# State part of an RWKV-7 mixer on 64x64 diagonal blocks, the convolution's chunks before the value's, ten of its taps on VectorE

## Chip, cores and metric

One core of a Trainium2 chip runs the whole program in one launch. The metric is device microseconds of that core, median of several executions. The engines named are TensorE (PE; PEld is its weight load), VectorE (DVE), ScalarE (ACT), GpSimd (POOL) and SyncE (SP, which issues the DMAs).

## What is computed

Two transformer layers on 256 tokens of width 1024, in float32. The first (attention, pooling mixer, gated feed-forward) is not touched. The second has a mixer of a causal depthwise convolution (512 channels, 31 taps) with layer norm and SiLU, and an RWKV-7 state of 8 heads of 64 channels, then a PEER feed-forward over 16384 experts. What the change touches is this part of the mixer:

```python
y = a * sigmoid(b)                     # 512 channels each, from w_in
y = depthwise_conv(y, w_dw) + b_dw     # 31 taps, causal
y_conv = silu(layernorm(y) * ln_w + ln_b)

def step(state, inp):                  # for each of 256 tokens, 8 heads, state 64x64
    r_t, k_t, v_t, w_t, kk_t, a_t = inp
    sa = einsum('bhij,bhj->bhi', state, -kk_t)
    state = state * w_t[:, :, None, :] + sa[..., None] * (kk_t * a_t)[:, :, None, :] \
            + v_t[..., None] * k_t[:, :, None, :]
    return state, einsum('bhij,bhj->bhi', state, r_t)
y = groupnorm(scan(step)) + bonus      # then * g, and concat(y_conv, y_rwkv) @ w_out
```

## The kernel before

Every large product goes over weight chunks of 128x1024 float32. SyncE loads them into a ring of four buffers (`raw`), ScalarE rounds each to `w_hi` (L497), VectorE subtracts to `w_lo` (L911, `split`), and TensorE makes three products of each 128x128 piece (L1511 to L1513). A chunk of the second layer's input projection (`MIX`, 22 chunks, `mix`) gives 128 channels x 256 tokens in one PSUM bank; ScalarE takes it out (`mix_taken`, L686) and VectorE adds the shifted token (`shift`, L1117). The order is lora inputs, k, r, v (chunks 10 to 13), the convolution's gates (14 to 17), its inputs (18 to 21). `conv_in` (L1188) is input times gate, in `cy`.

The state is computed in chunks of 64 tokens. A unit of work is a block b = 2t + h%2 (t: 128 tokens, that is two chunks; four heads k). First the factors Z, B, K and V are transposed to token-major (L1800) and taken out by ScalarE (`tok_major`, L736). The Gram products (L1814) of 128 tokens against 128 are masked by VectorE (L1208) to within 64x64 diagonal blocks, so that half of each 128x128 tile is zero. `NEUMANN` is a list of ten steps of one or two products that invert the triangular matrix; for each step, all four blocks: products (L1836, L1834 where a mask follows, L1832 a transpose) into banks 2b and 2b+1, evicted by ScalarE ("act", 36 of them, L759) or VectorE ("add", "copy", "eye" or a mask, 36, L1228, L1223, L1225, L1230). A block waits for its own evictions of the step before (`DONE`). Then m1 (L1843), m1T (L1848), w1 (L1854), m2 (L1860), phi (L1869) and u (L1877, L1878), the three rounds over chunk states (`phi_state`, L1891; L1903 `sa`), y (L1916, L1918, L1919), and y's group norm (L1923, L1761, L1769). Then the eight chunks of `w_out` (`W_OUT2`).

Beside the state part runs the convolution: ScalarE multiplies two tiles of 256 tokens by a tap's weight (`tap_pair`, L744, two instructions) into a ring of three pairs, GpSimd adds the pair to `co` (L1498). Sixty pairs are the 30 taps beyond the first; eight come in front of the Neumann loop, one or two behind each of ScalarE's evictions. The layer norm of `co` (sums on TensorE, L1885 and L1895) is issued among the chunk states. All engines work through their own queue in the order written; semaphores order them between each other. `w_out` chunks 3 to 7 are loaded after the Neumann loop, as D2U and D2L lie in `raw`.

## Time and profile before

| what | us |
|---|---|
| median of 3 runs | 1558.61 (1556.29 to 1560.1) |
| the profiled execution, its own time | 1559.9 |
| its span in the trace | 1558.1 |
| last chunk of the input projection ends | 544.0 |
| Gram products start | 548.7 |
| Neumann products | 554.8 to 626.6 |
| first chunk of `w_out` starts | 679.5 |

A row of a timeline has the start in us from the span's start, the length of the group, engine, line and operation, output and inputs, shapes, and how many records were merged; in brackets the idle time before it and what ended it. Each float32 matmul of TensorE leaves two records. Lengths of TensorE's records are modelled and overlap, so the distance between starts is what a record costs the engine. `PEclk` in a window is the granted clock as a share of 2.4 GHz.

### The profile page before, as it was taken

Reading aid. Unit: us, or ns where it says so; the run is one execution under the profiler, and the core shown is the slowest. Engines: PE = TensorE matmul, PEld = TensorE weight load, DVE = VectorE, ACT = ScalarE, POOL = GpSimd, SP = SyncE. Lnnn points to the kernel's source line nnn. Section 1 sums busy time; section 2 is a strip of 40 time slices with the busy share of each in tenths; the row PEclk is TensorE's granted clock in tenths of the full one; section 3 lists DMA queues with packets and bytes.
Section 4 is the critical chain, followed back from the end, with each engine's and each line's share of the span. In section 5 each row is a group of like instructions: output and inputs, shape, how many; then the busy total and the mean of one; then the engine's idle time right before and its main releaser. Section 6 shows DMA issues by size and latency. Waiting matters only on the chain.

```text
span 1558.1 us, 29537 instructions
## 1 busy us (share of the span) xinstructions
PE 1494.1 (96%) x10922; PEld 1367.6 (88%) x10922; DVE 1007.9 (65%) x1777; ACT 847.7 (54%) x1587; POOL 214.1 (14%) x128
## 2 busy tenths in 40 slices
PE   5999989999989999998999999999999999999997
PEld 5967979999969998888999999999999888888885
DVE  5454557665666764446996588888997555555554
ACT  5444546555546598334544456777775544544543
POOL 0030000000000089004788300000000000000000
PEclk9999999999999999999999999999999999999999
DMA  6545565666744400125556654444446666666661
GB/s 240 171 149 203 165 228 181 205 214 213 257 149 134 124 1 1 56 72 186 156 184 186 184 185 150 136 141 144 136 143 195 190 195 194 190 194 196 190 193 62
DMA packets 68365, 252.89 MB, mean 162 GB/s; under 512 B 7584, under 2 KB 7840, under 8 KB 67488
## 3 DMA queue, kind: packets, MB, share of 16 engines
q1 hardware_dynamic: 67104, 245.40, 49.6%
q10 hardware_dynamic: 1152, 5.98, 1.0%
q8 instruction: 76, 1.25, 0.3%
q14 instruction: 33, 0.27, 0.0%
HBM read 249.25 MB, written 2.10 MB: 161 GB/s over the span
## 4 chain that ended last, share of the span: by engine, by line
PE 89%; DVE 5%; ACT 3%; issue 3%; POOL 0%; DMA 0%; ACTq 0%; DVEq 0%; POOLq 0%
PE bank L2002 22%; PE bank L1511 18%; PE bank L1512 17%; PE bank L1513 17%; PE bank L1968 4%; PE bank L1544 2%; PE bank L1836 1%; DVE arena L932 1%; PE bank L1834 1%; DVE w_lo L911 1%; ACT arena L744 0%; PE bank L1953 0%; DVE arena L929 0%; POOL arena L1498 0%; PE bank L1559 0%
## 5 line engine op out<-in xcount | busy, mean ns | idle before, releaser
L1511 PE MATMUL bank<-x_hi,w_hi 128*128 128x256 f32 x2120 | 620.4, 293 | 19.2 <-DVE x_lo L942 6.3
L911 DVE TENSOR_TENSOR w_lo<-raw,w_hi 128x1024 fp32r<-128x1024 f32 x364 | 445.6, 1225 | 262.4 <-ACT w_hi L497 259.3
L1512 PE MATMUL bank<-x_lo,w_hi 128*128 128x256 f32 x2120 | 603.5, 285 | 0.0
L1513 PE MATMUL bank<-x_hi,w_lo 128*128 128x256 f32 x2120 | 603.2, 285 | 0.0
L497 ACT ACTIVATE w_hi<-raw 128x1024 fp32r<-128x1024 f32 x416 | 439.1, 1056 | 184.3 <-PE bank L2002 167.2
L1511 PEld LDWEIGHTS bank<-x_hi,w_hi 128*128 128x128 f32 x2120 | 409.8, 193 | 51.3 <-issue 36.3
L1512 PEld LDWEIGHTS bank<-x_lo,w_hi 128*128 128x128 f32 x2120 | 410.8, 194 | 0.4
L1513 PEld LDWEIGHTS bank<-x_hi,w_lo 128*128 128x128 f32 x2120 | 410.1, 193 | 0.0
L2002 PE MATMUL bank<-w_hi,x_hi 128*128 128x512 f32 x508 | 156.4, 389 | 0.0
L2002 PE MATMUL bank<-w_lo,x_hi 128*128 128x512 f32 x508 | 156.4, 389 | 0.0
L2002 PE MATMUL bank<-w_hi,x_lo 128*128 128x512 f32 x508 | 156.3, 389 | 0.0
L1473 POOL TENSOR_TENSOR w_lo<-raw,w_hi 128x1024 fp32r<-128x1024 f32 x52 | 125.3, 2411 | 120.6 <-ACT w_hi L497 120.6
L1498 POOL TENSOR_TENSOR arena<-arena 128x512 f32<-128x512 f32 x60 | 75.7, 1306 | 452.8 <-ACT arena L744 452.8
L2002 PEld LDWEIGHTS bank<-w_lo,x_hi 128*128 128x128 f32 x508 | 95.3, 188 | 19.9
L2002 PEld LDWEIGHTS bank<-w_hi,x_hi 128*128 128x128 f32 x508 | 95.3, 188 | 19.8
L2002 PEld LDWEIGHTS bank<-w_hi,x_lo 128*128 128x128 f32 x508 | 95.3, 188 | 19.8
L841 ACT ACTIVATE xres<-xres,i0T 128x128 f32<-128x128 f32 x256 | 81.9, 392 | 47.1 <-DVE xres L1380 47.1
L833 ACT ACTIVATE arena<-bank 128x256 f32<-128x256 f32 (+32 forms) x123 | 40.3, 328 | 88.9 <-PE bank L1513 88.8
L1380 DVE TENSOR_TENSOR xres<-kept,bank 128x1024 f32<-128x1024 f32 x64 | 78.0, 1220 | 16.2 <-PE bank L1968 16.2
L1968 PE MATMUL bank<-xres 128*128 128x128 f32 x512 | 67.6, 275 | 0.0
L1078 DVE SCALAR_TENSOR_TENSOR arena<-arena,vec 128x256 f32<-128x256 f32 x44 | 21.4, 486 | 67.7 <-ACT arena L656 67.6
L1968 PEld LDWEIGHTS bank<-xres 128*128 128x128 f32 x512 | 62.8, 192 | 0.0
(314 smaller groups left out, 1608.0 us busy)
## 6 DMA issues: line engine op xcount, KB each, us to landing
raw<-in_u SPq DMA_DIRECT2D x128, 512.0 KB, 3.6
raw<-in_v SPq DMA_DIRECT2D x128, 512.0 KB, 3.5
raw<-in_w_in SPq DMA_DIRECT2D x54, 512.0 KB, 4.3
arena<-in_ada SPq DMA_DIRECT2D x48, 512.0 KB, 4.6
raw<-in_w_up SPq DMA_DIRECT2D x44, 512.0 KB, 4.5
raw<-in_w_down SPq DMA_DIRECT2D x22, 512.0 KB, 3.7
raw<-in_w_out SPq DMA_DIRECT2D x16, 512.0 KB, 5.0
raw<-in_w_q SPq DMA_DIRECT2D x16, 512.0 KB, 3.6
```

The costliest lines, as they stand in the source:

```text
L497: act.activation(w_hi[:, s], raw[:, s], ACT.Copy).then_inc(hi_ready, 1)
L833: m = act.activation(h_chunk(n)[:, built // 4:], by_four(b[:, built:TOK]), ACT.Gelu)
L841: m = act.activation(hot[:, g % 2, 0, k], hot[:, g % 2, 0, k], ACT.Copy, scale=gT[:, 4 * g + k:4 * g + k + 1])
L911: dve.tensor_tensor(w_lo[:, s], raw[:, s], w_hi[:, s].bitcast(F32), ALU.subtract).then_inc(lo_ready, 1)
L1380: dve.tensor_tensor(hot[:, g % 2], iota.rearrange("p (c k s) -> p c k s", c=1, k=1).broadcast_to([P, 2, 4, 128]), e, ALU.is_equal)\
L1473: pool.tensor_tensor(w_lo[:, b % RING], raw[:, b % RING], w_hi[:, b % RING].bitcast(F32), ALU.subtract)\
L1498: pool.tensor_tensor(co[:, v], co[:, v], tap_product[:, 2 * (m % 3):2 * (m % 3) + 2], ALU.add).then_inc(S("tap_added"), 1)
L1511: pe.matmul(o, w, xh, start=start, stop=False, skip_group_check=True)
L1512: pe.matmul(o, w, xl, start=False, stop=False, skip_group_check=True)
L1513: return pe.matmul(o, wl, xh, start=False, stop=stop_, skip_group_check=True)
L1968: m = pe.matmul(bank[6 + g % 2][:, k * P:k * P + P], hot[:, g % 2, 0, k], hot[:, g % 2, 1, k], start=True, stop=True)
L2002: m = pe.matmul(bank[4 + 2 * a + half][:, :], left, right[:, s, half * 512:half * 512 + 512], start=begins, stop=ends, skip_group_check=True)
```

## The change

- **Blocks.** The four big matrices hold only the 64x64 diagonal blocks (128 x 64 for a pair of chunks, 1024 columns in place of 2048). Each product of 128x128 becomes two of 64x64: rows 0 to 63 of the array into partitions 0 to 63, rows 64 to 127 into 64 to 127, both into one bank. Evictions are 256 columns wide in place of 512. Masks are 64 wide, and `eye64` stands for the identity. The transpose in the loop becomes a product with the identity. D2U and D2L leave `raw`, so the `w_out` loads wait for nothing but the ring.
- **Banks.** The loop uses three pairs of banks (0 to 5) in turn; a job (one block of one step) waits for the evictions of the job three before it.
- **Order.** Chunks 10 to 17 are now the convolution's gates and inputs, 18 to 21 the value. The gates are kept raw and go through one sigmoid of 1024 columns. The transposes of Z, B, K and V stand between chunks 18 to 21, and eight tap pairs in front of the loop.
- **Taps.** Twenty taps (40 pairs) stay on ScalarE and GpSimd; ten (`own_tap`, 40 instructions of 256 columns) go to VectorE, into banks 6 and 7: four in front of the loop, one behind each of its 36 evictions. They are added to `co` after the sa additions.
- **Behind the loop.** w1 comes before m1T; phi and u use two banks each, read two chunks late; the layer norm of `co` is now behind the sa products, with the bonus gates (`bonus_gate`, before y's norm) and three `w_lo` splits on VectorE among it; y is made in two parts, the one on the chunk states first, in blocks of 64x64; ScalarE evicts y ahead of the convolution's SiLU.

```diff
+ACT_TAPS = 20
...
-            return U(2048).rearrange("p (b h s) -> p b h s", b=4, h=4)
+            return U(2048)[:, 0:1024].rearrange("p (b h s) -> p b h s", b=4, h=4)
 
         AK, RB, RK, EL, R_, DU, DL = (unit() for _ in range(7))
-        D2U, D2L = (raw[:, n:n + 2].rearrange("p r n -> p (r n)").rearrange("p (b h s) -> p b h s", b=4, h=4) for n in (0, 2))
+        D2U, D2L = (arena[:, PAST + n:PAST + n + 1024].rearrange("p (b h s) -> p b h s", b=4, h=4) for n in (1024, 3072))
+        HALF = [slice(0, 64), slice(64, 128)]
+
+        def neu_bank(s, b, k):
+            return bank[2 * ((4 * s + b) % 3) + k][:, 0:256]
+
+        def own_taps(f):
+            return bank[6 + f // 2][:, (f % 2) * TOK:(f % 2) * TOK + TOK]
...
             act.wait_ge(S("cum"), 5)
             act.activation(sw[:, :, :], sw[:, :, :], ACT.Exp, scale=-LAMBDA).then_inc(S("e3"), 1)
+            act.wait_ge(S("mix_taken"), 14)
+            act.activation(sgb[:, :, :], sgb[:, :, :], ACT.Sigmoid).then_inc(S("gated"), 1)
...
             act.wait_ge(S("conv_in"), 4)
-            for m in range(8):
-                tap_pair(m)
-            pair = 8
-            act.wait_ge(lo_ready, W_OUT2 + AHEAD)
+            pair = 0
+            for n in range(18, 22):
+                kept_part(n)
+                tap_pair(pair)
+                pair += 1
+                for t in range(2):
+                    token_major(2 * (n - 18) + t)
+            while pair < 8:
+                tap_pair(pair)
+                pair += 1
             for s, step in enumerate(NEUMANN):
                 for b in range(4):
                     for k, (lhs, rhs, dst, how) in enumerate(step):
                         if how != "act":
                             continue
                         act.wait_ge(S("neu_prod"), PROD[s, b, k])
-                        act.activation(MAT[dst][:, b].rearrange("p a b -> p (a b)"), bank[2 * b + k][:, :], ACT.Copy)\
+                        act.activation(MAT[dst][:, b].rearrange("p a b -> p (a b)"), neu_bank(s, b, k), ACT.Copy)\
                            .then_inc(S("neu_act"), 1)
-                        for _ in range(1 if pair < 20 else 2):
-                            if pair < 60:
-                                tap_pair(pair)
-                                pair += 1
-            for m in range(pair, 60):
-                tap_pair(m)
-
-            for t in range(2):
-                act.wait_ge(S("m1T_prod"), t + 1)
-                act.activation(m1T[:, :, t * 128:t * 128 + 128], bank[2 + t][:, :].rearrange("p (f s) -> p f s", f=4), ACT.Copy)\
-                   .then_inc(S("m1T"), 1)
+                        if pair < 2 * ACT_TAPS - 8 and (s, b) != (9, 3):
+                            tap_pair(pair)
+                            pair += 1
...
+            while pair < 2 * ACT_TAPS - 4:
+                tap_pair(pair)
+                pair += 1
...
+            dve.wait_ge(S("gated"), 5)
+            for n in range(4):
+                dve.wait_ge(chunk_used, MIX + 14 + n + 1)
+                own.after(dve.tensor_tensor(cy[:, n, 30:286], bank[n % 2][:, 0:TOK], sgb[:, n], ALU.mult))
+                dve.sem_inc(S("conv_in"), 1)
+                split(MIX + 14 + n + AHEAD)
+            split(MIX + 18 + AHEAD)
+            for f in range(4):
+                dve.tensor_scalar(co[:, f], cy[:, f, 0:256], V("conv_dw_w_2", 1, 31 * f), V("conv_dw_b_2", 1, f), ALU.mult, ALU.add)\
+                   .then_inc(S("own_taps"), 1)
+            for n in range(18, 22):
+                shift(n)
...
+            def own_tap(m):
+
+                tap, f = 1 + ACT_TAPS + m // 4, m % 4
+                src, w = cy[:, f, tap:tap + 256], V("conv_dw_w_2", 1, 31 * f + tap)
+                if m < 4:
+                    ins_ = dve.tensor_scalar(own_taps(f), src, w, None, ALU.mult)
+                else:
+                    dve.wait_ge(S("own_taps"), m + 1)
+                    ins_ = dve.scalar_tensor_tensor(own_taps(f), src, w, own_taps(f), ALU.mult, ALU.add)
+                ins_.then_inc(S("own_taps"), 1)
...
+            taps = 0
+            while taps < 4:
+                own_tap(taps)
+                taps += 1
...
+                        if taps < 4 * (30 - ACT_TAPS):
+                            own_tap(taps)
+                            taps += 1
...
+            dve.wait_ge(S("tap_added"), 2 * ACT_TAPS)
+            for f in range(2):
+                v = slice(2 * f, 2 * f + 2)
+                dve.wait_ge(S("own_taps"), 4 * (31 - ACT_TAPS))
+                own.mark(dve.tensor_tensor(co[:, v], bank[6 + f][:, :].rearrange("p (a t) -> p a t", a=2), co[:, v], ALU.add))
+            own.wait()
+            dve.sem_inc(S("conv_out"), 1)
+            for f in range(4):
+                bonus_gate(f)
+            own.wait()
+            dve.wait_ge(S("ln_mean"), 1)
+            for f in range(4):
+                dve.scalar_tensor_tensor(co[:, f], bank[1][:, 0:TOK], -1.0 / 512, co[:, f], ALU.mult, ALU.add).then_inc(S("ln_centred"), 1)
+            for n in range(19, 22):
+                split(MIX + n + AHEAD)
...
-            pool.wait_ge(S("conv_begun"), 4)
-            for m in range(60):
+            pool.wait_ge(S("own_taps"), 4)
+            for m in range(2 * ACT_TAPS):
...
+            def turn_factor(n, src):
+
+                if n == 0:
+                    pe.wait_ge(S("factors"), 1)
+                    pe.wait_ge(S("g_out"), 2)
+                if n == 3:
+                    pe.wait_ge(S("shifted"), 14)
+                for t in range(2):
+                    if n >= 2:
+                        pe.wait_ge(S("tok_major"), 2 * n - 3 + t)
+                    for f in range(4):
+                        m = pe.transpose(bank[(2, 3, 6, 7)[(2 * n + t) % 4]][:, f * P:f * P + P], src[:, f, t * P:t * P + P], ident)
+                    m.then_inc(S("turned"), 1)
+
             for n, src in enumerate((zf, bf, kf, xs[:, 10:14])):
-                if n == 3:
-                    pe.wait_ge(S("conv_in"), 4)
-                for t in range(2):
-                    for f in range(4):
-                        m = pe.transpose(bank[(2 * n + 2 + t) % 8][:, f * P:f * P + P], src[:, f, t * P:t * P + P], ident)
-                    m.then_inc(S("turned"), 1)
-            pe.wait_ge(S("tok_major"), 8)
-
+                mix(18 + n, 19 + n)
+                turn_factor(n, src)
...
+                    job = 4 * s + b
...
+                    if job >= 3:
+                        nd, na = EVICTED[job - 3]
                         if nd:
                             pe.wait_ge(S("neu_dve"), nd)
                         if na:
                             pe.wait_ge(S("neu_act"), na)
                     for k, (lhs, rhs, dst, how) in enumerate(step):
                         for u in range(4):
-                            o = bank[2 * b + k][:, u * P:u * P + P]
-                            if rhs == "turn":
-                                m = pe.transpose(o, MAT[lhs][:, b, u], ident)
-                            elif how[0] == "m":
-                                m = pe.matmul(o, fm(feat[lhs], b, u), fm(feat[rhs], b, u), start=True, stop=True)
-                            else:
-                                m = pe.matmul(o, MAT[lhs][:, b, u], MAT[rhs][:, b, u], start=True, stop=True)
+                            for c, rc in enumerate(HALF):
+                                o = neu_bank(s, b, k)[rc, u * 64:u * 64 + 64]
+                                if rhs == "turn":
+                                    m = pe.matmul(o, MAT[lhs][rc, b, u], ident[rc, rc], start=True, stop=True)
+                                elif how[0] == "m":
+                                    m = pe.matmul(o, fm(feat[lhs], b, u, c), fm(feat[rhs], b, u, c), start=True, stop=True)
+                                else:
+                                    m = pe.matmul(o, MAT[lhs][rc, b, u], MAT[rhs][rc, b, u], start=True, stop=True)
                         m.then_inc(S("neu_prod"), 1)
...
+            def per_head(t):
+
+                for h in range(8):
+                    for rc in HALF:
+                        yield 2 * t + h % 2, h // 2, rc, slice(h * 64, h * 64 + 64)
+
             for t in range(2):
-                for h in range(8):
-                    b, k = 2 * t + h % 2, h // 2
-                    m = pe.matmul(bank[t][:, h * 64:h * 64 + 64], R_[:, b, k], zt[:, t, h * 64:h * 64 + 64], start=True, stop=True)
+                for b, k, rc, v in per_head(t):
+                    m = pe.matmul(bank[t][rc, v], R_[rc, b, k], zt[rc, t, v], start=True, stop=True)
                 m.then_inc(S("m1_prod"), 1)
...
+            def y_place(h, t, c):
+
+                f, r = h // 2, HALF[h % 2]
+                return bank[4 * c][r, f * P + t * 64:f * P + t * 64 + 64]
 
             for h in range(8):
-                r, f = slice(64 * (h % 2), 64 * (h % 2) + 64), h // 2
+                for t in range(2):
+                    for c, rc in enumerate(HALF):
+                        r, f, at = HALF[h % 2], h // 2, t * P + 64 * c
+                        m = pe.matmul(y_place(h, t, c), st[r, 2 * t + c, f], rf[r, f, at:at + 64], start=h < 2 and t == 0, stop=False,
+                                      skip_group_check=True)
+            m.then_inc(S("y_prod"), 1)
+            pe.wait_ge(S("ln_sq"), 4)
+            for f in range(4):
+                m = pe.matmul(bank[1][:, 0:TOK], ones, cy[:, f, 0:TOK], start=f == 0, stop=f == 3)
+            m.then_inc(S("ln_var"), 1)
+            pe.wait_ge(S("y_prod"), 1)
...
+                    for left, right in ((sa, RB), (vt, RK)):
+                        for c, rc in enumerate(HALF):
+                            m = pe.matmul(y_place(h, t, c), left[rc, t, v], right[rc, b, k], start=False, stop=left is vt, skip_group_check=True)
```

## Rows read from the trace of the kernel before

**Rows 1.** The page: its first line, and TensorE in its part 1 (busy us, share, instructions).

```profile
span 1558.1 us, 29537 instructions
PE 1494.1 (96%) x10922; PEld 1367.6 (88%) x10922; DVE 1007.9 (65%) x1777; ACT 847.7 (54%) x1587; POOL 214.1 (14%) x128
```

**Rows 2.** Windows of the state part: window, length, busy us by engine, clock, DMA share, GB/s.

```profile
548.70:554.70 6.00, 5.03 (x64) 4.84 (x64) 4.06 (x6) 5.05 (x13) 5.10 (x5) 1.00 0.00 0
554.70:626.60 71.90, 68.25 (x560) 64.56 (x560) 34.56 (x46) 63.45 (x144) 70.60 (x56) 1.00 0.01 1
626.60:644.20 17.60, 17.57 (x320) 17.25 (x320) 5.46 (x11) 2.39 (x4) 0.00 (x0) 1.00 0.34 121
644.20:653.00 8.80, 6.76 (x117) 5.40 (x113) 4.91 (x14) 4.38 (x7) 0.00 (x0) 1.00 0.01 2
653.00:668.30 15.30, 15.28 (x128) 11.40 (x128) 6.61 (x15) 3.30 (x8) 0.00 (x0) 1.00 0.00 1
668.30:679.50 11.20, 8.00 (x57) 7.02 (x57) 5.52 (x10) 3.94 (x6) 0.00 (x0) 0.77 0.01 1
```

**Rows 3.** Timeline, TensorE: start, length of the group in us, operation, shapes, records.

```profile
544.02 3.65 PE L1800 MATMUL bank<-kept,arena 128*128 128x128 f32 x32
578.25 7.41 PE L1836 MATMUL bank<-arena 128*128 128x128 f32 x64
644.25 1.99 PE L1885 MATMUL bank<-arena,kept 128*128 128x256 f32 x8
648.55 0.68 PE L1891 MATMUL bank<-arena 64*64 64x64 f32 x16 [1.69 <-DVE arena L1264]
651.08 1.56 PE L1903 MATMUL bank<-arena 64*64 64x64 f32 x64
653.01 0.41 PE L1916 MATMUL bank<-arena 64*64 64x64 f32 x4 [0.36 <-DVE arena L1269]
```

**Rows 4.** Timeline, GpSimd, the additions of taps.

```profile
549.60 46.14 POOL L1498 TENSOR_TENSOR arena<-arena 128x512 f32<-128x512 f32 x36 [452.27 <-ACT arena L744]
596.25 29.56 POOL L1498 TENSOR_TENSOR arena<-arena 128x512 f32<-128x512 f32 x24 [0.51 <-ACT arena L744]
```

**Rows 5.** Timeline, ScalarE: a copy and what follows; eviction and tap pair in the loop.

```profile
530.98 0.39 ACT L686 ACTIVATE arena<-bank 128x256 f32<-128x256 f32 x1 [1.55 <-PE bank L1513]
531.26 1.05 ACT L497 ACTIVATE w_hi<-raw 128x1024 fp32r<-128x1024 f32 x1
605.76 0.58 ACT L759 ACTIVATE arena<-bank 128x512 f32<-128x512 f32 x1
607.41 0.91 ACT L744 ACTIVATE arena<-arena,vec 128x256 f32<-128x256 f32 x2 [0.28 <-POOL arena L1498]
608.23 0.58 ACT L759 ACTIVATE arena<-bank 128x512 f32<-128x512 f32 x1
```

**Rows 6.** Timeline, VectorE: shift, split, R's start, an eviction of 256 columns.

```profile
521.52 0.48 DVE L1117 SCALAR_TENSOR_TENSOR arena<-bank,vec,arena 128x255 f32<-128x255 f32 x1
521.92 1.22 DVE L911 TENSOR_TENSOR w_lo<-raw,w_hi 128x1024 fp32r<-128x1024 f32 x1
559.12 5.98 DVE L1213 TENSOR_TENSOR arena<-arena,kept 128x512 f32<-128x512 f32 x4
640.25 1.42 DVE L1243 TENSOR_TENSOR arena<-bank,arena 128x256 f32<-128x256 f32 x4 [3.50 <-PE bank L1869]
```

**Rows 7.** Windows where the granted clock fell: columns as in rows 2.

```profile
446.00:450.00 4.00, 1.51 (x9) 1.31 (x8) 3.07 (x7) 1.89 (x3) 0.00 (x0) 0.88 0.70 193
450.00:454.00 4.00, 4.00 (x26) 3.60 (x28) 1.04 (x2) 0.96 (x2) 0.00 (x0) 0.70 0.69 228
672.00:676.00 4.00, 2.50 (x18) 2.42 (x20) 1.48 (x4) 2.35 (x3) 0.00 (x0) 0.79 0.00 0
676.00:680.00 4.00, 4.00 (x35) 3.67 (x34) 2.87 (x7) 0.72 (x2) 0.00 (x0) 0.50 0.02 4
```

215 lines of the change are left out of this document (98 added, 117 removed).

## Prediction

> **What bounds the kernel now.** The page comes first: TensorE is busy 96% of the span [rows 1], so all loops over weights are its own, and the change leaves them alone. What it touches is the state part between the last input-projection chunk (ends 544.0) and the first `w_out` chunk (starts 679.5), 135.5 us. Cut into windows [rows 2] it reads: 72 us of Neumann products, with TensorE busy 68 of them; 17.6 for m1, m1T, w1, m2, phi and u; 8.8 for the chunk states, in which the convolution's layer norm is threaded; 15.3 for y; 11.2 for y's group norm. The timeline of TensorE gives the price of one record (each float32 matmul is two): I take the time from start to start, which is (length of the group minus one record's own length) / (records minus 1). For 128x128 blocks that is (7.41 - 0.28)/63 = 0.113 us [rows 3]. 560 records x 0.113 = 63 us of the 72. The other engines have slack here by this view, but not on the tap chain: GpSimd adds 60 tap pairs in 549.6 to 625.8 [rows 4], almost the whole Neumann stretch, so it is a second bound right under TensorE. Both have to shrink, and the change shortens both.
>
> **The change, part by part.**
>
> *Tiles.* Each 128x128 product becomes two of 64x64 on the diagonal quarters: 72 Neumann products of 16 records, 1152 in all (before 560). No row shows this stream at length. Nearest is `phi_state` (L1891), also row half r into column half r of one bank: (0.68 - 0.22)/15 = 0.031 us [rows 3]. Ends: two halves into two banks (L1903), (1.56 - 0.22)/63 = 0.021; four records of one quarter (L1916, 0.41 us), (0.41 - 0.23)/3 = 0.060 [rows 3]. I take 0.030, as the nearest row has the same placement. A product then takes 0.48 us, a block with two products (a job) 0.96.
>
> *Order of the chunks.* Until the end of chunk 17 (530.8; ScalarE takes it at 530.98 [rows 5]) TensorE does the same work. Then: bonus sums 1.9 and four chunks of 2.88, as before, with 24 of the 32 transposes (3.65 us [rows 3]) between them, so chunk 21 ends at about 546.8. The value's copy and shift are now behind it: 0.39 + 0.48 us [rows 5, 6] and hand-offs, 1.1; its 8 transposes 0.9. The Gram products start at 548.9 (before, at 548.7, where the first window begins [rows 2]). Their masks are 256 wide: 0.42 + 0.16 hand-off each instead of 0.69 + 0.16, so the first Neumann product can start at about 553, before 554.8. Gain 1.7. The sigmoid of the gates is one table load and one wide instruction on ScalarE's queue with the w_hi splits 17 to 20 behind it; TensorE holds chunks 14 to 16 ready (8.6 us), which covers its 2.3 us. DVE's conv inputs move in front of the shifts with their four w_lo splits; same count, same cover.
>
> *Taps.* GpSimd now adds 40 pairs instead of 60. Its cadence is 29.56/24 = 1.23 us (and 46.14/36 = 1.28 in the stretch that has contention) [rows 4]. The convolution input is complete 11.5 us earlier, so four pairs are done beside the last chunks, and four from 550 to 553.4. ScalarE's own cost in the loop is an eviction (0.48 at 512 wide; at 256 wide about 0.28, as in the copy after which the next instruction starts 0.28 later) plus a pair (607.41 to 608.23, 0.82) [rows 5] = 1.10, under GpSimd's 1.23. So Neumann steps 0 to 3 (20 ScalarE evictions, 20 pairs) go at GpSimd's pace: pair number n is added by 550.9 + 1.23(n - 3), the ring of three lets ScalarE be three ahead, so the last eviction of step 3 comes at 550.9 + 1.23 x 21 = 576.8, plus 1.0 because the four two-SBUF-input additions that start R hold GpSimd up (5.98 us for four at 512 wide [rows 6], half of that here): 577.8. From there:
> - step 4, VectorE: 8 evictions and 8 own taps. Evictions 0.33 apart (L1243, (1.42 - 0.42)/3); a tap is a scalar_tensor_tensor on 256 columns, like the shift after which VectorE goes on 0.40 later [rows 6]. 8 x 0.73 = 5.8, half of it ahead of 577.8: +3.
> - steps 5, 6, 7: two products per job, TensorE 4 x 0.96 = 3.84 against VectorE's 4 x 0.73 and, in step 5, ScalarE's 4.4: 4.4 + 3.8 + 3.8 = 12.
> - step 8: VectorE 4 x 0.73 = 2.9. Step 9: 4 x 0.48, drain and last eviction, 2.5.
> End of Neumann: 577.8 + 3 + 12 + 2.9 + 2.5 = 598.2; before 626.6. **Gain 28.4.**
> What I don't know here: an own tap writes and re-reads PSUM while GpSimd runs. Lower end 0.33 like an eviction; upper end 0.75, a quarter of the 5.98 us halved [rows 6]. That moves the sum by -0.6 to +6.
>
> *Behind the loop.* m1, w1, m2: 64 records each at 0.030 = 5.8, m1T 64 at 0.021 = 1.3: 7.1 (before 12.9). ScalarE has four tap pairs (3.3) between m1T and m2, so m2 is in SBUF only at +10.4; phi hides under that, u starts then and takes 3.3: +13.7 (before +17.6). States: u0 is read two chunks late because c and c+2 share a bank (1 us), then two rounds and the sa products as before: that window took 8.8, of which the norm's two sums, 2.0 each (L1885 [rows 3]), were about 1.7 more than the states needed: 13.7 + 1 + 7.1 = +21.8. Now the convolution's norm comes on the path: two additions of own taps 1.4, mean 2.0, then the bonus gates (8 instructions at 0.40 of L1117 [rows 6], 3.2, of which 2.0 beside the mean), centring 4 x 0.33, square 0.4, variance 2.0, to about +30.5. y: 64 records on st hide under the centring, 128 records at 0.021 to 0.030 end at +34.2. Before, y took 15.3 [rows 2] for 128 records that changed between tile shapes. Three w_lo splits on VectorE (L911, 1.2 each [rows 6]) stand in front of the norm's reciprocal and hide under variance and y. The group norm took 11.2 [rows 2]; its square now has the silu of four tiles in front of it on ScalarE, +1.1: 34.2 + 12.3 = **+46.5**; before 679.5 - 626.6 = 52.9. **Gain 6.4.**
>
> *Nothing on the path:* the mask copy (L1234 of after, about 0.5 us on VectorE while chunk 0 runs), the `w_out` loads that no longer wait for the loop (the ring holds them anyway), the shared semaphore in the q/k norm.
>
> **Sum.** 28.4 + 6.4 = 34.8 us (the 1.7 is in the first). I give back 2 for hand-offs that a pipeline with three jobs in flight won't hide: 33. The profiled execution took 1559.9 (span 1558.1), 1.3 above the median of 1558.6; 1559.9 - 33 = 1526.9, and 1.3 less for a median, say **1526**. All after 679.5 is TensorE at 90% or more and moves up whole.
> Bounds: records at 0.021 take 5 off. At 0.045, steps 1 to 3 become TensorE's (17.3 for 14.8), steps 5 to 7 5.3 longer, 8 and 9 2, the 192 behind 2.9: +13. Dear taps +6. The conv norm worse than threaded +7. Together 1516 to 1546.
>
> **Where a page speaks against it.** L1891's two row halves write one bank at 0.031 us, where L1903's, in two banks, need 0.021 [rows 3]. The Trainium skill, "TensorEngine Tiling (Array Packing)", Restrictions and Gotchas, says that different row tiles cannot access the same PSUM bank simultaneously, and this change writes both halves of each block to one bank. By that rule the halves take turns, which is the first rival. The trace agrees only with a third of it: slower than two banks, but twice as fast as one quarter alone.
>
> **Rivals.**
> 1. *The halves take turns* (chance 0.10). 0.060 us a record, L1916 [rows 3]. Steps 1 to 3: 12 jobs x 1.92 = 23 for 14.8; step 4 +3; steps 5 to 7 23 for 12; 8 and 9 +2.4; behind +5.8. In sum +31: 1557. The whole gain is gone; it turns to a loss past 0.062. Against it: L1891 at length 16.
> 2. *The clock falls* (0.06), the slower end. In step 0 TensorE has 3.8 us of work in 9. The granted clock was 0.88 and then 0.70 around a stretch busy 1.5 of 4 us, and 0.79 and then 0.50 where 2.5 of 4 were busy [rows 7]. If the loop runs at 1.2 of 2.4 GHz, records cost 0.060 (rival 1, +31) and y, mean, variance and spread double where they are on the path (+14): 1571. It decides once half clock lasts beyond step 3; if only for step 0, it costs nothing, as GpSimd paces that. Against it: the clock was 1.00 in all windows but the last, also among the chunk states, busy 6.8 of 8.8 us [rows 2].
> 3. *The gain in the loop comes, the one behind it not* (0.12): VectorE, now with taps, gates, centring, splits and reciprocal in one queue, keeps y waiting. Tail 54 for 46.5: 1534.
> The change does what it says: placement is in the addresses.
>
> **Chances.** Forecast 0.72, rival 3 0.12, rival 1 0.10, rival 2 0.06. Range 1515 to 1546 holds the first two and the dear ends of the unknowns. About 0.3% (4.7 us) is what can be told from no change. Faster by more 0.89 (forecast, rival 3, half of rival 1); same 0.04; slower 0.07.
>
> **What would show it.** In the windows of after: Neumann from about 553 to 598; GpSimd without gaps until step 4; records 0.030 apart; VectorE 0.73 for eviction and tap; m1 to u 14 us; from the loop's end to `w_out` 46. Wrong if TensorE is busy throughout steps 1 to 7 (rival 1), if PEclk falls under 0.9 in the loop (rival 2), or if ln_mean to y exceeds 12 us (rival 3).

## The result: 1522.6 us, 36.6 less, and the profile after

| | before | after |
|---|---|---|
| median, us (lowest to highest) | 1559.23 (1556.29 to 1560.10), 4 runs | 1522.64 (1521.17 to 1524.25), 4 runs |
| ratio, 95% interval | 1 | 0.9769 (0.975 to 0.9787) |
| profiled execution (span) | 1559.9 (1558.1) | 1521.37 (1519.5) |

The forecast was 1526. The page of the kernel after, the first lines of its parts 1 and 2 (busy us, share; tenths of 40 slices). Beside [rows 1] TensorE is busy 44 us less. GpSimd's (POOL) additions of taps are the 7 and the 5 in slices 15 and 16, each 38 us long; its digits from slice 18 on lie behind the state part:

```profile
span 1519.5 us, 31129 instructions
PE 1449.6 (95%) x11770; PEld 1328.0 (87%) x11770; DVE 1010.1 (66%) x1820; ACT 824.5 (54%) x1548; POOL 189.0 (12%) x108
POOL 0030000000000075017787000000000000000000
```

Windows of the kernel after, cut at its own stages (chunks and transposes; Gram products; Neumann loop; m1 to u; states and sa; norm and y; y's group norm). They answer to [rows 2], with the same columns:

```profile
526.51:544.61 18.10, 17.01 (x139) 16.42 (x137) 7.06 (x13) 12.23 (x23) 4.62 (x4) 1.00 0.30 95
544.61:548.58 3.97, 2.74 (x129) 2.60 (x128) 2.69 (x7) 3.93 (x10) 2.90 (x3) 1.00 0.03 6
548.58:592.13 43.55, 38.79 (x1152) 37.12 (x1152) 36.80 (x86) 31.98 (x84) 32.92 (x27) 0.92 0.02 4
592.13:606.80 14.67, 12.31 (x448) 12.03 (x448) 5.14 (x11) 8.75 (x20) 7.51 (x7) 1.00 0.01 3
606.80:616.90 10.10, 4.69 (x96) 4.16 (x96) 5.64 (x14) 0.00 (x0) 2.39 (x2) 0.58 0.01 2
616.90:628.40 11.50, 11.42 (x208) 9.67 (x208) 9.84 (x17) 3.10 (x6) 0.00 (x0) 0.77 0.30 106
628.40:640.80 12.40, 7.86 (x63) 6.75 (x59) 6.76 (x14) 8.33 (x15) 0.00 (x0) 0.80 0.08 32
```

The reader is to see three things. The loop is 43.55 us where it was 71.8, and no single engine fills it: TensorE 38.8, VectorE 36.8, GpSimd 32.9. Behind it TensorE idles more than half of the states' stretch (4.69 of 10.1). And from the states on the granted clock is 0.58 to 0.80, where it was 1.00 up to y's group norm and 0.77 in it [rows 2].

The difference of the two profiled executions, 38.5 us, by the starts of the same TensorE instructions:

| stretch | before | after | difference |
|---|---|---|---|
| up to the projections in front of the change (`lora_sb`, L1794 of after) | 488.33 | 485.38 | -2.95 |
| from there to the bonus sums | 42.45 | 41.13 | -1.32 |
| bonus sums to the first Neumann product | 24.00 | 22.07 | -1.93 |
| Neumann loop (first product to m1) | 71.84 | 43.55 | -28.29 |
| m1 to the first `w_out` chunk | 52.8 | 48.7 | -4.1 |

The first row is none of the change's doing: TensorE's instructions there are the same. In the window from 30 to 60 us the clock was granted at 0.89 in the one execution and 0.94 in the other. In after and the eleven kernels below whose code is equal up to that point it is reached at 484.09 and 484.97 where that window had 1.00, at 485.36 to 486.95 with 0.94, and at 486.94 to 488.60 with 0.89. So the trace overstates the change by about 2 us, and the medians (-36.6) are the better number.

### The profile page after: what moved, and what is told of

Same layout as the page of the kernel before. It is cut to its first block, busy times and chain, and to the rows that moved or that the text cites. A ratio compares the mean times of both kernels' runs of the same rounds, so it can differ in the third digit from the quotient of the medians.

```text
span 1519.5 us, 31129 instructions
## 1 busy us (share of the span) xinstructions
PE 1449.6 (95%) x11770; PEld 1328.0 (87%) x11770; DVE 1010.1 (66%) x1820; ACT 824.5 (54%) x1548; POOL 189.0 (12%) x108
## 3 DMA queue, kind: packets, MB, share of 16 engines
q10 hardware_dynamic: 1152, 5.98, 1.0%
## 4 chain that ended last, share of the span: by engine, by line
PE 90%; DVE 4%; ACT 2%; issue 2%; POOL 1%; DMA 0%; ACTq 0%; DVEq 0%; POOLq 0%
PE bank L2079 23%; PE bank L1557 18%; PE bank L1558 18%; PE bank L1559 18%; PE bank L2045 4%; PE bank L1590 2%; PE bank L1898 2%; DVE arena L948 1%; POOL arena L1546 1%; PE bank L2030 0%; DVE arena L945 0%; PE bank L1605 0%; DVE w_lo L927 0%; DMA vec<-in_vec 0%; PE bank L1817 0%
## 5 line engine op out<-in xcount | busy, mean ns | idle before, releaser
L2079 PEld LDWEIGHTS bank<-w_hi,x_hi 128*128 128x128 f32 x508 | 95.3, 188 | 19.7
L1546 POOL TENSOR_TENSOR arena<-arena 128x512 f32<-128x512 f32 x40 | 50.3, 1298 | 463.2 <-ACT arena L751 463.2
```

What stands on the lines that cost most here:

```text
L1546: pool.tensor_tensor(co[:, v], co[:, v], tap_product[:, 2 * (m % 3):2 * (m % 3) + 2], ALU.add).then_inc(S("tap_added"), 1)
L2079: m = pe.matmul(bank[4 + 2 * a + half][:, :], left, right[:, s, half * 512:half * 512 + 512], start=begins, stop=ends, skip_group_check=True)
```

## Experiments

Medians of each kernel, the ratio to the kernel before on the same chip in the same job, and two stretches of its profiled execution: the loop (first Neumann product to m1) and the tail (m1 to the first `w_out` chunk).

| kernel | median, us | ratio (95%) | loop | tail |
|---|---|---|---|---|
| before | 1559.23 | 1 | 71.84 | 52.8 |
| before, no pairs | 1554.27, one run | | 68.04 | 52.8 |
| after | 1522.64 | 0.9769 (0.975 to 0.9787) | 43.55 | 48.7 |
| no pairs | 1512.52 | 0.9697 (0.9682 to 0.9711) | 35.16 | 46.9 |
| taps back | 1545.37 | 0.9917 (0.9901 to 0.9932) | 69.15 | 45.3 |
| identity in PSUM | 1523.55 | 0.9773 (0.9759 to 0.9786) | 41.71 | 50.3 |
| m2 first | 1521.35 | 0.9755 (0.9741 to 0.9768) | 43.30 | 48.9 |
| unread matmuls | 1523.68 | 0.9761 (0.9743 to 0.978) | 42.45 | 51.0 |
| pairs in the loop | 1517.53 | 0.9733 (0.972 to 0.9746) | 40.10 | 46.9 |
| norm early | 1518.15 | 0.9729 (0.9716 to 0.9742) | 43.13 | 48.2 |
| norm early, five buffers | 1513.66 | 0.9704 (0.9691 to 0.9717) | 41.02 | 41.8 |
| m2 first, buffers, unread matmuls | 1516.56 | 0.9725 (0.9712 to 0.9738) | 40.75 | 47.9 |
| norm early, buffers, unread matmuls | 1512.23 | 0.9694 (0.9681 to 0.9707) | 40.32 | 40.7 |

**1. What a 64x64 matmul costs, and the first rival.** Streams of 32 matmuls each in front of the state products of after, for example A and C:

```
+ for i in range(32):
+     pe.matmul(bank[0][HALF[i % 2], v], R_[HALF[i % 2], b, k], zt[HALF[i % 2], 0, v], start=True, stop=True)
+ m.then_inc(S("probe"), 1); pe.wait_ge(S("probe"), 1)
...
+     pe.matmul(bank[0][0:64, v], R_[0:64, b, k], zt[0:64, 0, v], start=True, stop=True)
```

> The kernel after, with six streams of 32 matmuls of 64x64 by 64 columns (64 records with the weight loads) ahead of phi_state, each stream behind a wait on the one before, so that the trace shows each by itself; their products are not used. A: rows and columns alternate between the halves of the array, one PSUM bank. B: the same, two banks. C: one quarter of the array, one bank. D: rows fixed, columns alternate, one bank. F: rows alternate, columns fixed, two banks. G: all four quarters in turn, two banks. What the prediction rests on (the two halves run beside each other whatever the bank, and the record is the price): A, B and G alike at 0.02 to 0.031 us a record, 1.3 to 2.0 us a stream, C at twice that or more. The rival (two row halves that write one bank wait for each other): A at twice B and like C. The clock's level in each stream has to be read beside it, for TensorE is idle before the first.

TensorE's instructions grouped by line (records | busy us, mean ns | idle before): L1956 is A, L1961 B, L1971 D.

```profile
L1956 PE MATMUL bank<-arena 64*64 64x64 f32 x64 | 4.0, 312 | 0.0
L1961 PE MATMUL bank<-arena 64*64 64x64 f32 x64 | 2.3, 232 | 0.1
L1971 PE MATMUL bank<-arena 64*64 64x64 f32 x64 | 2.1, 220 | 0.1
```

The timeline of C (L1966), F (L1976) and G (L1981), and windows in A, C and G:

```profile
610.69 3.94 PE L1966 MATMUL bank<-arena 64*64 64x64 f32 x64
...
616.84 2.08 PE L1976 MATMUL bank<-arena 64*64 64x64 f32 x64
618.99 1.16 PE L1981 MATMUL bank<-arena 64*64 64x64 f32 x64
```

```profile
606.00:608.00 2.00, 2.00 (x40) 2.00 (x36) 0.71 (x2) 0.00 (x0) 0.59 (x1) 0.50 0.00 0
...
612.50:614.50 2.00, 2.00 (x37) 1.99 (x35) 0.00 (x0) 0.00 (x0) 0.00 (x0) 1.00 0.00 0
...
618.50:620.50 2.00, 1.84 (x88) 1.57 (x84) 0.00 (x0) 0.00 (x0) 0.00 (x0) 1.00 0.00 0
```

From start to start at full clock (one record's own length taken off, then 63 steps), one quarter alone takes (3.94 - 0.22)/63 = 0.059 us a record, two quarters in turn (2.08 - 0.22)/63 = 0.030, four (1.16 - 0.22)/63 = 0.015. Which two makes no difference: rows in common (D, one bank), columns in common (F, two banks), neither (B, of whose 2.3 us a part ran at half clock). A, the change's own pattern with both halves in one bank, took 4.0 at half clock, which would be 2.0 at full: like F in two banks. After's own m1 shows the same at clock 1.00: 64 records, each 32 of them with both halves in one bank, start at 592.13 and the next group at 594.05, 0.030 a record. **Rival 1 is out.** The Trainium skill, "TensorEngine Tiling (Array Packing)", Restrictions and Gotchas, has the rule that different row tiles can't access one PSUM bank at the same time; here two row tiles that write different partitions of one bank lost nothing. Two row tiles that write the same partitions of one bank were not tried. So 0.030 is no issue price of a record but the occupation of a quarter, shared among the quarters in use. L1903 [rows 3] goes through all four quarters, 16 records on one pair and 16 on the next, and its 0.021 lies between the price of two and of four; two banks by themselves gained nothing here. The loop uses two of four.

**2. GpSimd and ScalarE out of the way.** Of after:

```
 def tap_pair(m):
+    if True:
+        return
...
-dve.wait_ge(S("tap_added"), 2 * ACT_TAPS)
...
-for m in range(2 * ACT_TAPS):
+for m in range(0):
```

> The kernel after without the 20 taps that ScalarE multiplies and GpSimd adds; that part of the convolution is left out, and all else stays. By the prediction GpSimd's pace costs the first steps of the loop only: the loop of products would fall from 43.6 us to TensorE's own 896 records, 0.0277 to 0.030 each and a little of hand-over, that is 36 to 40, and the four additions that start R from 5.62 us to 4 x 0.42 = 1.7 if it is GpSimd's additions that stand between them, and stay at 5.6 if their length is their own (the operands in SBUF). With m2 no more behind tap pairs and no conv wait, the tail from the end of the loop to w_out falls by 1 to 3 from 48.8. In all 1508 to 1514. The rival, that the loop is TensorE's alone and GpSimd costs it nothing: loop 43 to 44, the kernel 1518 to 1521.

The same was done to before:

> The kernel before, without the 30 taps that ScalarE multiplies and GpSimd adds; that part of the convolution is left out. The prediction says that before's loop was TensorE's own, 560 records of 128x128 at 0.113 us, 63 of the 71.8, and that the pairs were a second bound under it. So: first product to m1 in 65 to 71 us against 71.8, the four additions that start R at 2.7 or less instead of 5.98, and the kernel at 1551 to 1558 (before 1559). If instead the pairs paced it, as they do after, the loop falls to 63 to 65 and the kernel under 1551.

The additions that start R on VectorE (L1245 of after, L1247 here; timeline: start, length of the group, instructions), first of after, then of after without the pairs:

```profile
551.32 5.62 DVE L1245 TENSOR_TENSOR arena<-arena 128x256 f32<-128x256 f32 x4
```

```profile
552.89 1.43 DVE L1247 TENSOR_TENSOR arena<-arena 128x256 f32<-128x256 f32 x4
```

The window of before's loop without the pairs:

```profile
552.98:621.02 68.04, 67.35 (x560) 64.26 (x561) 31.26 (x46) 21.50 (x36) 0.00 (x0) 1.00 0.00 1
```

After's loop falls from 43.55 to 35.16 and the kernel by 10 us; the four additions are 4.2 us shorter. In before the pairs cost 3.8 us (71.84 to 68.04), and TensorE is busy 67.35 of the 68.04 us left. So with no pairs on either side the blocks are worth 32.9 us of loop, although after still has its own taps on VectorE, and the pairs give 4.6 of it back. Before's expectation held: 65 to 71 for the loop, and the four additions that start R took 2.50 (expected 2.7 or less). After's loop fell a little further than the 36 to 40 expected; the kernel (1508 to 1514) came as expected.

**3. The taps put back** (30 on ScalarE and GpSimd, none on VectorE, blocks as in after):

```
-ACT_TAPS = 20
+ACT_TAPS = 30
...
-if pair < 2 * ACT_TAPS - 8 and (s, b) != (9, 3):
-    tap_pair(pair)
+for _ in range(1 if pair < 20 else 2):
+    if pair < 60:
+        tap_pair(pair)
...
-while taps < 4:
+while False:
     own_tap(taps)
```

The two additions of own taps into `co` are left out with them.

> The kernel after with the taps as they were: all 30 by ScalarE's pairs and GpSimd's 60 additions, none on VectorE; the 64x64 blocks stay. By the prediction GpSimd's 60 additions at 1.23 to 1.25 us, 75 us from 532, set the end: the last at about 611 or later instead of 609.2, two more pairs after m2, the loop at the pace of pairs (two in a place from the twentieth on) 50 to 60 us instead of 43.6, and the kernel at 1528 to 1540. The rival, that VectorE's own taps cost the loop as much as they save: the loop within 2 us of 43.6 and the kernel within 3 of after's 1522.6.

Timeline of GpSimd in that kernel, then the window of its loop:

```profile
546.21 40.08 POOL L1542 TENSOR_TENSOR arena<-arena 128x512 f32<-128x512 f32 x32 [1.07 <-ACT arena L751]
587.15 29.47 POOL L1542 TENSOR_TENSOR arena<-arena 128x512 f32<-128x512 f32 x24 [0.86 <-ACT arena L751]
```

```profile
548.56:617.71 69.15, 51.88 (x1153) 48.97 (x1153) 22.96 (x46) 56.44 (x140) 67.20 (x55) 0.70 0.01 2
```

56 additions stand with one gap of 0.86 us between them, up to 616.62, and m1 starts 1.1 us later. The loop is 69.15, a mere 2.7 less than before's 71.84, with TensorE at 64x64, at a mean clock of 0.70, and still idle for 17 of the 69 us. The loop and the kernel, at 1545.4, are both outside what I expected (50 to 60, and 1528 to 1540): I had named the 60 additions and not carried their sum to the end, 70.4 us from 546.2. **In the loop the smaller blocks are worth next to nothing as long as GpSimd has 60 additions**: 2.7 us, against 28.3 with 40. What this kernel still gains on before, 14 us, lies mostly around the loop: 1.3 and 1.9 ahead of it as in after, and 7.5 in the tail, whose products are in 64x64 too and which has neither the own taps' additions nor tap pairs ahead of m2.

**4. The four additions.** Identity copied to PSUM, so that only one operand comes from SBUF:

```
+own.after(dve.tensor_copy(bank[6][:, 256:320], C("eye64", 64)))
+eye = bank[6][:, 256:320].rearrange("p (a s) -> p a s", a=1).broadcast_to([P, 4, 64])
 for b in range(4):
-    dve.tensor_tensor(R_[:, b], DU[:, b], mask("eye64"), ALU.add).then_inc(S("neu_start"), 1)
+    dve.tensor_tensor(R_[:, b], eye, DU[:, b], ALU.add).then_inc(S("neu_start"), 1)
+dve.wait_ge(S("neu_start"), 4)
```

> The kernel after with the 64x64 identity copied to a PSUM bank first, and the four additions that start R reading it there. Theory A (VectorE and GpSimd take turns where both operands are in SBUF, one GpSimd addition per VectorE addition): the four take 0.4 to 0.5 us each instead of 1.46, GpSimd's beside them stay at 1.23 instead of 1.40, TensorE's idle time of 1.7 us ahead of step 1 goes, and the kernel is faster by 1 to 3 us. Theory B (the length comes from the broadcast read or the strides): they stay over 1 us each and the time is within 0.5 us. Theory C: the additions shorten but GpSimd's pace is next, and the time gains under 1 us.

```profile
551.18 1.42 DVE L1247 TENSOR_TENSOR arena<-bank,arena 128x256 f32<-128x256 f32 x4
```

1.42 us for four instead of 5.62, with GpSimd busy 10.00 of the 10 us from 548 on: it is the pair of SBUF operands beside GpSimd, for without GpSimd the same pair took 1.43 (experiment 2). The Trainium skill, "SBUF — State Buffer", SBUF: two separate sides, says just this: VectorE with two SBUF inputs and GpSimd take an exclusive lock on one port pair for a whole instruction each. The trace agrees: (5.62 - 1.49)/3 = 1.38 from start to start with the last one's own 1.49 taken off, about one GpSimd addition (1.24) each. The loop is 1.84 shorter than in after, but part of that is the clock: the kernel with the unread matmuls (experiment 6) has after's loop, instruction for instruction, and ran it at 1.00 in 42.45. The windows of the two loops:

```profile
550.13:592.58 42.45, 37.37 (x1152) 35.13 (x1152) 36.91 (x86) 31.98 (x84) 32.93 (x27) 1.00 0.01 4
```

```profile
548.18:589.89 41.71, 37.39 (x1153) 35.13 (x1153) 33.32 (x87) 31.83 (x84) 32.19 (x27) 1.00 0.01 4
```

At one clock the edit gives 0.74 us of loop, although VectorE is busy 3.6 us less: the four additions stood beside GpSimd's pace, which is what the next steps wait for. Even the 0.74 isn't firm, for the two kernels with the early norm and five buffers (experiment 7) have one loop and ran it, both at 1.00, in 41.02 and 40.32. So theory C is the one that stands. The kernel did not get faster (1523.55 against 1522.64, intervals that overlap): in the profiled execution the tail is 1.7 longer, 1.2 of it from u to the first state, with the clock at 0.69 already in 600 to 606, where after had 1.00. The edit changes nothing there, so this is a loss that goes with the clock.

**5. m2 evicted in front of the tap pairs.**

```
-while pair < 2 * ACT_TAPS - 4:
-    tap_pair(pair)
-    pair += 1
 for t in range(2):
     act.wait_ge(S("m2_prod"), t + 1)
```

> The kernel after with one order changed: ScalarE evicts m2 before it multiplies the four tap pairs that stand ahead of it, not behind them. Theory A (u waits for m2 behind the pairs, 1.80 us of TensorE idle): the u products start 1.5 to 2 us sooner after the loop's end than the 10.5 of after, and the kernel is faster by 1 to 2. Theory B (the convolution's wait, ahead of its norm, takes its place, for the pairs end later): u is sooner and the norm is not, the kernel within 0.7 us.

The u products started 8.3 us after m1 instead of 10.5, and then nothing came of it. VectorE's state additions tell why (GpSimd, then VectorE, of this kernel):

```profile
602.59 10.08 POOL L1543 TENSOR_TENSOR arena<-arena 128x512 f32<-128x512 f32 x8 [19.19 <-ACT arena L751]
...
607.48 1.45 DVE L1290 COPY arena<-arena 128x256 f32<-128x256 f32 x1
...
610.25 1.30 DVE L1296 TENSOR_TENSOR arena<-arena 128x256 f32<-128x256 f32 x1
...
613.24 0.42 DVE L1296 TENSOR_TENSOR arena<-arena 128x256 f32<-128x256 f32 x1
```

The copy and the first addition, while GpSimd adds, take 1.45 and 1.30 us; the second addition, after GpSimd's end at 612.67, takes 0.42. It is the wait of experiment 4, moved onto the path of the states: against after's 0.40 and 0.43 the two cost 1.9 of the 2.2 us won, and the sa products start 20.1 us after m1 in both kernels. The median is 1.3 lower and the ratios' intervals overlap. So theory A's gain didn't come, and theory B's reason (the norm's wait) wasn't it either.

**6. The clock in the tail.** Matmuls that nobody reads, where TensorE waits; the eight stand ahead of the states and again ahead of the norm's mean:

```
+def keep_busy(n):
+    for _ in range(n):
+        pe.matmul(bank[1][:, 256:384], ones, ident, start=True, stop=True)
+keep_busy(8)
...
 m.then_inc(S("phi_state"), 1)
+keep_busy(4)
```

> The kernel after with matmuls that nobody reads (128x128 by 128 columns, a free bank) at TensorE's waits in the tail: 8 ahead of the state products, 4 after each phi_state, 8 ahead of the convolution's norm. Theory A (the tail's missing gain is the granted clock, which falls where TensorE is idle from 606.8 on: y1 3.26 against 1.97, m1-to-w_out 48.8 where 46.5 was forecast): the clock stays near 1.00 in those stretches, the norm's eight sums go from 3.78 to 2.0 and the y products from 3.3 to 2.0, and the kernel is faster by 2 to 5 us. Theory B (VectorE's and ScalarE's hand-overs set the tail): the clock is higher but the kernel is within 1 us. Theory C: the extra matmuls delay the chain, slower by 0 to 2.

> The kernel after with m2 evicted first, the identity in PSUM, five tap buffers, and the unread matmuls in the tail (8 ahead of the states, 4 after each, 8 ahead of the norm). Where only the unread matmuls were put in, they stood behind u's wait of 1.80 us, the clock was at half level when they ran and they took what they gave. Here u has no such wait. Theory A (they keep the clock if it has not fallen yet): granted clock 0.95 or more from u to y2, the tail from the end of the loop to w_out 43 to 46, the kernel at 1511 to 1516. Theory B (the clock falls all the same, as it did with u early): tail 48 to 51 and the kernel at 1516 to 1521.

Windows of the tail: alone (two lines), then with m2 first, the PSUM identity and five buffers (three lines, the first from m1 to sa):

```profile
603.07:611.65 8.58, 8.58 (x144) 8.34 (x144) 2.08 (x6) 3.36 (x8) 6.53 (x6) 0.60 0.01 4
611.65:624.00 12.35, 11.56 (x201) 10.30 (x200) 9.29 (x23) 0.44 (x2) 0.00 (x0) 1.00 0.01 2
```

```profile
590.89:610.35 19.46, 17.46 (x513) 16.69 (x513) 10.37 (x18) 8.77 (x20) 10.11 (x8) 1.00 0.01 3
610.35:618.00 7.65, 7.45 (x140) 6.70 (x141) 6.30 (x16) 0.00 (x0) 0.00 (x0) 1.00 0.01 3
618.00:638.77 20.77, 14.56 (x211) 12.11 (x205) 12.92 (x21) 11.40 (x21) 0.00 (x0) 0.81 0.23 77
```

Alone they ran at clock 0.60 and gained nothing: from u to the first state it is 8.6 us (in after 5.6), the u products among it 4.6 instead of 3.3, and the kernel stayed where it was. In the second kernel the clock is 1.00 up to 618, and yet from the start of the sa products to `w_out` it takes 638.77 - 610.35 = 28.4 us, as in after (640.8 - 612.3 = 28.5, clock 0.50 in 612 to 618). Its tail (47.9) and the kernel (1516.6) are nearer to theory B (48 to 51, 1516 to 1521) than to A (43 to 46, 1511 to 1516). The sa products, the mean and the variance show where the clock's gain went, first in after, then in the second kernel:

```profile
612.27 2.60 PE L1964 MATMUL bank<-arena 64*64 64x64 f32 x64 [0.98 <-DVE arena L1299]
616.98 3.78 PE L1970 MATMUL bank<-arena,kept 128*128 128x256 f32 x8 [2.11 <-DVEq L1313]
623.88 1.99 PE L1987 MATMUL bank<-arena,kept 128*128 128x256 f32 x8
```

```profile
610.35 1.56 PE L1976 MATMUL bank<-arena 64*64 64x64 f32 x64 [0.86 <-DVE arena L1304]
614.10 1.99 PE L1983 MATMUL bank<-arena,kept 128*128 128x256 f32 x8 [0.20 <-DVEq L1318]
620.24 3.60 PE L2000 MATMUL bank<-arena,kept 128*128 128x256 f32 x8 [1.53 <-ACT arena L796]
```

In after the clock is 0.50 for sa and the mean and 1.00 for the variance; in the second kernel it is 1.00 for the first two and 0.53 for the variance (620.24 to 623.76). Sa and the mean are 2.8 us shorter there. VectorE's queue of additions and gates covers a part of it: the centring starts 7.0 us after the start of sa instead of 8.6. The other 1.6 us is lost again in the variance, 3.60 long instead of 1.99, and the second part of y starts 13.4 us after sa (in after 13.5). So the unread matmuls moved the stretch at half clock and didn't remove it. **That the clock costs the tail nothing is not shown; that these matmuls win it back isn't either.** No kernel with the norm behind sa ran sa, mean and variance all at full clock; by these numbers it would have about 1.6 us to win, an estimate.

**7. GpSimd out of the tail, the norm early, and both.** All pairs go into the loop; the tap products get five buffers instead of three, in a region that is free by then. M2 comes first and the identity is in PSUM, as in experiments 4 and 5:

```
-if pair < 2 * ACT_TAPS - 8 and (s, b) != (9, 3):
+if pair < 2 * ACT_TAPS and (s, b) != (9, 3):
...
-if m >= 3:
-    act.wait_ge(S("tap_added"), m - 2)
+if m >= 5:
+    act.wait_ge(S("tap_added"), m - 4)
```

> The kernel after with m2 evicted first, the identity in PSUM, five tap buffers and all tap pairs inside the loop; the convolution's norm stays where after has it. It separates the two things that the best kernel has in its tail: GpSimd out of it, and the norm early. With m2 first alone, the state's copy and additions on VectorE, both operands in SBUF, took 1.30 to 1.45 us instead of 0.42 while GpSimd added, and the tail was no shorter. Theory A (GpSimd's additions beside the states are what the tail loses): copy 0.27 to 0.40, additions 0.42, u to the first state in 5.6 to 6.2 us, the end of the loop to w_out in 44.5 to 46.5 where after has 48.7, and the kernel at 1516 to 1519. Theory B (the norm's place is what counts): that stretch stays at 47.5 or more, and the kernel at 1519 to 1522 in spite of a loop 2 us shorter.

GpSimd, then the state's copy and additions on VectorE:

```profile
547.75 44.36 POOL L1551 TENSOR_TENSOR arena<-arena 128x512 f32<-128x512 f32 x36 [1.07 <-ACT arena L756]
...
604.11 0.29 DVE L1298 COPY arena<-arena 128x256 f32<-128x256 f32 x1
...
606.12 0.42 DVE L1304 TENSOR_TENSOR arena<-arena 128x256 f32<-128x256 f32 x1
...
608.22 0.42 DVE L1304 TENSOR_TENSOR arena<-arena 128x256 f32<-128x256 f32 x1
```

Copy and additions are short, the tail is 46.9 (m2 first alone 48.9; theory A expected 44.5 to 46.5), the loop 3.4 us shorter, the kernel at 1517.5: inside theory A's range, and 5 us under after. How much of the loop's part is the buffers', the identity's or the pairs' place was not separated. The norm's order, with m2 first and all pairs in the loop but three buffers and the identity in SBUF:

```
+pe.wait_ge(S("conv_out"), 1)
+for f in range(4):
+    m = pe.matmul(bank[6][:, 0:TOK], ones, co[:, f], start=f == 0, stop=f == 3)
+m.then_inc(S("ln_mean"), 1)
 pe.wait_ge(S("phi"), 4)
...
 dve.tensor_copy(st[:, 1], u0[:, 0]).then_inc(S("state"), 1)
+dve.wait_ge(S("ln_mean"), 1)
+for f in range(4):
+    dve.scalar_tensor_tensor(co[:, f], bank[6][:, 0:TOK], -1.0 / 512, co[:, f], ALU.mult, ALU.add).then_inc(S("ln_centred"), 1)
```

The same lines go from behind the states; the variance moves ahead of y in the same way, the additions of own taps behind the copies of w1, and three splits of weights on VectorE ahead of the states.

> The kernel after with the tail in another order: all tap pairs inside the loop of products, m2's evictions straight behind m1T's, the two additions that join VectorE's taps right behind the copies of w1, the norm's mean (bank 6) ahead of the state products, its centring behind the first state, its variance (bank 7) behind sa, and three splits of weights moved ahead of all that. Theory A (the tail is a chain of hand-overs in which the convolution's norm stands behind the states): from the end of the loop to w_out 38 to 42 us instead of 48.8, the loop longer by 0 to 2 for its 8 more pairs, and the kernel at 1512 to 1518 against after's 1522.6. Theory B (the granted clock, at half level for TensorE's idle time, takes the gain back): the tail is 44 to 47 and the kernel at 1518 to 1522. Theory C: the pairs in the loop make GpSimd its pace, loop up by 4 or more and no gain in all.

> The kernel with the norm's work early and all tap pairs in the loop, and with two more changes: the identity in PSUM for the additions that start R, and five buffers for the tap products instead of three, so that ScalarE can run ahead of GpSimd. Theory A (what is left of GpSimd in the loop, 43.6 us against 35.2 without it, is ScalarE held by a full ring and the four additions): the loop falls to 37 to 41 us, GpSimd without a gap, the kernel at 1510 to 1516. Theory B (GpSimd's sum is what counts, 36 additions at 1.23 from 546 on, however many buffers): the loop ends no sooner than with three, 1515 to 1519.

> The kernel with the norm's work early, the identity in PSUM and five tap buffers, and four unread matmuls after each state product. Against the same kernel without them: by theory A (the clock is what is left in the tail) the granted clock of the stretch from sa to y2 is 0.9 or more and the kernel is 2 to 4 us faster; by theory B (it fell in the u products already, and the extra matmuls run at half clock) the two are within 1.5 us.

Windows from sa to `w_out`, first the early norm with five buffers, then the same with the unread matmuls:

```profile
610.15:632.88 22.73, 17.99 (x321) 15.82 (x321) 13.20 (x27) 8.94 (x17) 0.00 (x0) 0.82 0.01 1
```

```profile
611.14:632.73 21.59, 17.36 (x322) 15.55 (x321) 13.11 (x27) 8.91 (x17) 0.00 (x0) 0.85 0.01 2
```

From sa to `w_out` it is 22.7 us instead of 28.5: the mean, the centring and the square now lie beside the states. The first kernel with this order had its five runs spread over 8 us (1515.74 to 1523.59), and its profiled one, the slowest, has the clock at 0.53 from 606 to 624, with 7.8 us from the first u product to the norm's mean; there the norm's sums stand in the states' way and the clock does count. Its tail, 48.2 in that execution, fits none of the three theories, and its median lies at the edge of A and B.

With the identity in PSUM and five buffers it is 1513.66 (expected by theory A 1510 to 1516). This kernel and "pairs in the loop" differ in the norm's place alone, with the additions and the splits that go with it, so the pair gives the price of that place: the tail 41.8 instead of 46.9, and the kernel 3.9 us faster (ratios 0.9704 and 0.9733, intervals apart). With the unread matmuls it is 1512.23, the fastest kernel, 47 us under before and 10 under after (ratios 0.9694 and 0.9769, intervals apart). Against the same kernel without them that is 1.4 us, which theory B allowed (1.5), with intervals that overlap; that the matmuls help is not shown. (In its profiled execution sa and variance took 0.4 and 1.2 us less than without them, at full clock, and the stretch to `w_out` 1.1 less.) Theory B of the buffers said no sooner than 43.1; the loop is 41.0, of which the PSUM identity alone may give up to 1.8. What the buffers give by themselves was not separated, and neither theory is shown by it.

## Why the prediction was right, step by step

- **Record price 0.030**: right. m1's 64 records start at 592.13, the next group at 594.05. Its reason was wrong (experiment 1): not an issue price but one quarter's occupation. The number came out right by luck, because the row that I took had the same placement and so the same two quarters in use. (Rival 1's own sum comes to 30.4, not 31, which changes nothing.)
- **Rival 1**: refuted by stream A. **Rival 2**: the clock did fall, to 0.50 in 558 to 564 and to 0.58 to 0.80 behind the loop. I had given it 0.06 and 1571 if it stayed low beyond step 3. It did not. In the loop it cost about 1 us at most: 43.55 at a mean of 0.92, 42.45 for the same loop at 1.00, and 42.59 and 43.30 for two executions of it at 0.96. Behind the loop it lengthened sa by 1.0 us and the mean by 1.8 (experiment 6), of which VectorE's queue covers a part; my forecast had both at full clock. **Rival 3** (tail 54) did not come.
- **Order of the chunks**: -1.93 for a forecast of -1.7, read from the two traces; no run changes the order alone. What I did not see is the 1.32 in front: in before TensorE waits 0.92 us at 522.06 for VectorE's shift (L1117) and 0.24 at 510.34, and after has no such waits in those places.
- **GpSimd's pace**: 24 additions in 30.29 us, 1.26 each (1.23 forecast). With both executions on one clock (2.95 + 1.32 us earlier, 4.3), step 3 was forecast to end at 573.5; its last eviction starts at 572.44. From there to m1 it is 19.7 us, forecast 20.4.
- **VectorE's 0.73** for an eviction and a tap: taps start at 575.16, 575.88 and 576.60 with an eviction between each two, 0.72. So the loop was forecast at 45.2 and measured 43.55, and the 2 us that I handed back for hand-overs were not needed.
- **The additions that start R, mis-sized**: I took half of before's 5.98 for half the width, about 3.0. They took 5.62, 2.6 more. Beside GpSimd width was not the price; one GpSimd addition for each was (experiments 2 and 4). The sum holds only 1.0 for them, as what they hold GpSimd up, and that was about right: its 24 additions took 30.29 for 24 x 1.23 = 29.5. In the loop's length the whole wait weighs 1.8 at most (experiment 4), since GpSimd's additions go on beside it.
- **Tail 46.5, measured 48.7**: u is at +10.5 as forecast (behind the pairs). Sa is done at +22.7 for +21.8; its products took 2.60 at clock 0.50, and 1.56 where the clock was 1.00. From there it takes 25.9 for 24.7; the mean in it took 3.78 at 0.50 where I had 2.0, and the gates beside it cover a part. How the 1.2 divides between the clock and the additions and the norm on VectorE was not separated. I had not seen that GpSimd's last eight additions (599.29 to 609.20) lie beside the states; in after only the copy runs beside them, and it took 0.40, so there they cost little. They cost as soon as u comes earlier (experiment 5).
- **Sum**: forecast -33, measured by medians -36.6. Of the 3.6: 1.3 from the unseen waits, 1.8 from the loop with the stretch ahead of it (28.3 + 1.9 for 28.4), 2 not handed back, less 2.3 in the tail (a gain of 4.1 for 6.4), makes 2.8; 0.8 is within the spread of the runs. So the total lies as near as it does partly because these misses have both signs.

## What to carry to other kernels

When two resources stand one close under the other, cost them as a pair: smaller blocks on TensorE saved 2.7 us of loop as long as GpSimd had 60 additions, and 28 with 40. Look for every VectorE instruction with two SBUF operands that can run beside GpSimd; it costs a GpSimd instruction, and a broadcast constant in PSUM or another time for GpSimd frees it. And move work that only feeds a later norm beside a chain of hand-overs rather than behind it: that made the tail 5.1 us shorter and the kernel 3.9 us faster (experiment 7), where taking the tap pairs out of m2's way alone changed nothing that can be told.

## What the runs showed of the hardware that was not expected

- 64x64 float32 matmuls of 64 columns at full clock, two records each: 0.118 us in one quarter, 0.059 with two quarters in turn, 0.030 with four.
- A VectorE addition of 256 columns: 0.42 us alone, 1.30 to 1.49 beside GpSimd's additions when both inputs are in SBUF, 0.42 beside them with one input in PSUM. A copy from SBUF to SBUF took 0.29 alone and 0.40 to 1.45 beside them.
- The clock at half level lengthened two sums of 8 records of 128x128 by 256 columns alike, 1.99 to 3.78 and 3.60, and where one of them was spared the other was hit.
- Before the change's code is reached, equal code starts up to 4.5 us apart from one execution to another (484.09 to 488.60), with the granted clock in 30 to 60 us at 1.00 to 0.89. And one loop took 41.02 and 40.32 us at one clock. A difference of 1 us can't be read from two traces without a look at that.
